# Hybrid decoder layer on Trainium2: laying the queries out through DRAM instead of by many small copies

## What is computed

```python
z = u @ w_in
qa, ka, va, qn, kc, vc, ksl, vsl, kw, vw, g_nsa, g_merge = jnp.split(z, cuts, axis=-1)
qa = rope(heads_q(qa, A_KV_HEADS, A_REP), pos)
ka = rope(heads_kv(ka, A_KV_HEADS), pos)
oa = banded_attention(qa, ka, heads_kv(va, A_KV_HEADS), A_WINDOW, sinks...)
qn_rot = rope(qn, pos)
kcmp = compress(heads_kv(kc, ...), ...)      # gelu(flat @ w1 + b1) @ w2
vcmp = compress(heads_kv(vc, ...), ...)
o_cmp, p_cmp = compressed_attention(qn, kcmp, vcmp)
idx = select_blocks(p_cmp)
o_slc = selected_attention(qn_rot, rope(ksl), vsl, idx)
o_win = banded_attention(qn_rot, rope(kw), vw, B_WINDOW, None)
y = gm[:, :, 0] * (oa @ w_proj_a) + gm[:, :, 1] * (ob @ w_proj_b)
h  = layer_norm(ALPHA * x + y @ w_out)
x' = layer_norm(ALPHA * h + (silu(h @ w_gate) * (h @ w_up)) @ w_down)
```

## Time and profile before

| | |
|---|---|
| runs of the kernel | 4864.35, 4977.32, 5441.69 us (median 4977.32) |
| profiled execution, time | 4870.62 us |
| profiled execution, span of the slowest core (core 6) | 4869.6 us |
| spans of all cores | 4842.0 to 4869.6 us |
| mean granted TensorE clock | 0.972 to 0.975 of full speed |
| busy, share of the span | PE 88%, weight loads 43%, DVE 41%, ACT 36%, POOL 20% |
| DMA | 413 MB, mean 85 GB/s |

### The profile page before, as it was taken

The page is one execution under the profiler, slowest core; times in us unless marked ns, Lnnn a source line. Parts: engine busy times, 40 slices in busy tenths (PEclk is TensorE's granted clock), DMA queues, the critical chain, the costliest instruction groups (busy, mean ns, idle before and its releaser), DMA issues.

```text
span 4869.6 us, 82285 instructions; the slowest of 8 cores (4842.0 to 4869.6 us)
## 1 busy us (share of the span) xinstructions
PE 4304.5 (88%) x27000; PEld 2112.4 (43%) x27000; DVE 2004.3 (41%) x4848; ACT 1746.9 (36%) x2186; POOL 989.3 (20%) x891
## 2 busy tenths in 40 slices
PE   2777899899987889999997789999999688999998
PEld 1344444344444444444443444444444344444444
DVE  0554455232355445523145544542325544453323
ACT  0158723211125862321122685331111388333111
POOL 1431112210243111102034210210114311121101
PEclk6899999999999999999999999999999999999999
DMA  7240133945222011253421101234432110124231
GB/s 126 76 106 14 24 107 94 213 125 156 81 71 74 2 53 53 93 165 89 131 80 54 61 2 53 78 104 139 129 97 86 46 46 2 74 74 156 89 122 45
DMA packets 207375, 412.99 MB, mean 85 GB/s; under 512 B 33008, under 2 KB 80496, under 8 KB 203760
## 3 DMA queue, kind: packets, MB, share of 16 engines
q1 hardware_dynamic: 173952, 356.97, 22.0%
q0 software_dynamic: 33008, 50.77, 6.9%
HBM read 327.79 MB, written 99.14 MB: 88 GB/s over the span
## 4 chain that ended last, share of the span: by engine, by line
PE 71%; ACT 8%; DMA 5%; SPq 5%; DVE 5%; issue 4%; POOL 1%; DVEq 0%; POOLq 0%; ACTq 0%
PE bpair L317 23%; PE bpair L318 12%; PE bpair L315 9%; ACT pt L340 7%; SPq L156 5%; PE bpair L316 5%; PE bpair L302 4%; PE bpair L307 4%; PE bpair L314 4%; PE bpair L309 2%; PE bpair L308 2%; PE bpair L335 1%; DMA ffr<-wu 1%; PE bpair L312 1%; DVE pre L344 1%
## 5 line engine op out<-in xcount | busy, mean ns | idle before, releaser
L317 PE MATMUL bpair<-hT,ffr 128*128 128x512 bf16 x5632 | 1229.9, 380 | 24.5 <-DMA ffr<-wg 17.3
L340 ACT ACTIVATE pt<-bpair 128x1024 bf16<-128x1024 f32 (+1 forms) x1016 | 991.9, 1018 | 230.3 <-PE bpair L313 129.3
L317 PEld LDWEIGHTS bpair<-hT,ffr 128*128 128x128 bf16 x5632 | 549.7, 98 | 691.0 <-issue 38.7
L344 DVE TENSOR_TENSOR actf<-sgt,bpair 128x512 bf16<-128x512 f32 x352 | 240.8, 688 | 914.3 <-PE bpair L317 896.2
L318 PE MATMUL bpair<-Wd,actf 128*128 128x512 bf16 x2816 | 609.1, 379 | 0.0
L340 ACT ACTIVATE sgt<-bpair 128x512 f32<-128x512 f32 x352 | 207.7, 596 | 834.0 <-PE bpair L317 833.5
L315 PE MATMUL bpair<-xT,wgm 128*128 128x512 bf16 x2048 | 488.8, 382 | 0.0
L318 PEld LDWEIGHTS bpair<-Wd,actf 128*128 128x128 bf16 x2816 | 275.5, 98 | 332.2
L302 PE MATMUL bpair<-xT,w 128*128 128x512 bf16 x1664 | 393.9, 393 | 28.5 <-DVE t L344 14.1
L307 PE MATMUL bpair<-Qr,Ksl 128*128 128x512 bf16 x1088 | 344.9, 387 | 75.9 <-ACT pt L340 49.8
L344 POOL TENSOR_TENSOR sb_lnst<-sb_lnst,sb_mhalf 128x1 f32<-128x1 f32 x128 | 70.2, 549 | 1501.3 <-DVE sb_lnst L350 1501.3
(11 more groups left out here) (130 smaller groups left out, 4589.1 us busy)
## 6 DMA issues: line engine op xcount, KB each, us to landing
ffr<-wg_b SPq DMA_DIRECT2D x154, 256.0 KB, 3.0
ffr<-wu_b SPq DMA_DIRECT2D x154, 256.0 KB, 3.2
pre<-x SPq DMA_DIRECT2D x64, 512.0 KB, 3.8
hs<-pre SPq DMA_DIRECT2D x64, 512.0 KB, 2.6
H<-hs SPq DMA_DIRECT2D x64, 512.0 KB, 4.3
out<-H SPq DMA_DIRECT2D x64, 512.0 KB, 2.6
Wd<-wd_b SPq DMA_DIRECT2D x66, 256.0 KB, 4.5
xT<-xt POOLq DMA_DIRECT2D x16, 1024.0 KB, 12.5
```

The source lines that it names most:

```text
L317: "gu": lambda *a, **k: t.matmul(*a, **k),
L340: return self.s.op("act", lambda: nc.scalar.activation(out=out, in_=in_, func=func, **kw), reads, writes, war)
L344: return self.s.op(eng, lambda: e.tensor_tensor(out=out, in0=in0, in1=in1, op=op), reads, writes, war, out.shape[0])
```

## The change

Five edits: the queries of both mixers go, tile by tile of 128x512, into a DRAM tensor `qd` and are read back from it in the wanted layout, one write and one read where there were four copies (`lay_out`); the Bufs of `QaT`, `Qn` and `Qr` are split by half; mixer A's key copies are issued by ACT, with a Buf `b_ka` of their own; `compress1` runs behind each of the first four pairs of query projections instead of behind every second; the sinks have a Buf of their own, and their exponential stands behind the keys of the first sequence.

```diff
-            dsems = {q: [... for i in range(16)] for q in ("sp", "pool")}
+            dsems = {q: [... for i in range(16)] for q in ("sp", "pool", "act")}
...
+        self.qd = self.nc.dram_tensor("qd", [48, 128, 512], BF16, kind="Internal").ap()
+        self.b_qd = [Buf("qd%d" % i) for i in range(48)]
...
-        s.dma("sp", (self.esink[:], dr["sinks"]), writes=[bc])
-        self.act(self.esink[:], self.esink[:], AF.Exp, [bc], [bc])
+        self.b_sink = Buf("sink")
+        s.dma("sp", (self.esink[:], dr["sinks"]), writes=[self.b_sink])
...
+    def lay_out(self, place, src, bs, dst, b_dst):
+
+        self.s.dma("sp", (self.qd[place], src), reads=[bs], writes=[self.b_qd[place]])
+        self.s.dma("sp", (dst, self.qd[place].rearrange("(j p) t -> p j t", j=4)), reads=[self.b_qd[place]],
+                   writes=[b_dst])
...
-            prs = []
-            for h in range(2):
-                for g in range(2):
-                    prs.append((self.KaT[64 * g + 32 * h:64 * g + 32 * h + 32, g, ts_], o[h][32 * g:32 * g + 32, :]))
-                    prs.append((self.Ksl[32 * h:32 * h + 32, g, ts_], o[h][64 + 32 * g:96 + 32 * g, :]))
-            s.dma("sp", prs, reads=bo, writes=[self.b_k1[tc]])
+            hg = [(h, g) for h in range(2) for g in range(2)]
+            s.dma("sp", [(self.Ksl[32 * h:32 * h + 32, g, ts_], o[h][64 + 32 * g:96 + 32 * g, :]) for h, g in hg],
+                  reads=bo, writes=[self.b_k1[tc]])
+            s.dma("act", [(self.KaT[64 * g + 32 * h:64 * g + 32 * h + 32, g, ts_], o[h][32 * g:32 * g + 32, :])
+                          for h, g in hg], reads=bo, writes=[self.b_ka[tc]])
...
         if not self.cbias_done:
             self.cbias_done = True
+            self.act(self.esink[:], self.esink[:], AF.Exp, [self.b_sink], [self.b_sink])
...
-                s.dma("sp", [(self.QaT[64 * g + 32 * h:64 * g + 32 * h + 32, j, ts_], o[h][32 * j:32 * j + 32, :])
-                             for h in range(2) for j in range(4)], reads=bo, writes=[self.b_qa[g][tc]])
-                if g == 1:
-                    compress1(tc // 2, tc % 2)
+                for h in range(2):
+                    self.lay_out(8 * g + 2 * tc + h, o[h][:], bo[h], self.QaT[64 * g + 32 * h:64 * g + 32 * h + 32, :, ts_],
+                                 self.b_qa[g][tc][h])
+                if tc < 2:
+                    compress1(tc, g)
...
-            s.dma("sp", [(self.Qn[64 * g + 32 * h:64 * g + 32 * h + 32, j, ts_], zq[h][32 * j:32 * j + 32, :])
-                         for j in range(4)], reads=[b_zq[h]], writes=[self.b_n[g][tc]])
+            self.lay_out(16 + 8 * g + 2 * tc + h, zq[h][:], b_zq[h], self.Qn[64 * g + 32 * h:64 * g + 32 * h + 32, :, ts_],
+                         self.b_n[g][tc][h])
...
-                s.dma("sp", [(self.Qr[g][32 * e:32 * e + 32, j, ts_], o[e][32 * j:32 * j + 32, :])
-                             for e in range(2) for j in range(4)], reads=bo, writes=[self.b_q[g][tc]])
+                for e in range(2):
+                    self.lay_out(32 + 8 * g + 2 * tc + e, o[e][:], bo[e], self.Qr[g][32 * e:32 * e + 32, :, ts_],
+                                 self.b_q[g][tc][e])
```

More of the change, by code:

```diff
@@ L397, in build @@
             sems = {e: E(nc.semaphore("s_" + e)) for e in Sched.ENG}
-            dsems = {q: [E(nc.semaphore("d_%s%d" % (q, i))) for i in range(16)] for q in ("sp", "pool")}
+            dsems = {q: [E(nc.semaphore("d_%s%d" % (q, i))) for i in range(16)] for q in ("sp", "pool", "act")}
             self.s = Sched(nc, sems, dsems)
@@ L572, in phase_p @@
         self.b_one = Buf("one", spans=span(M_V, 12480))
-        self.b_k1 = [Buf("k1_%d" % i, spans=span(M_KA + 1024 * i, 1024, 0, 64) + span(M_KA + 4096 + 1024 * i, 1024, 64, 128)
-                         + strided(M_KS + 1024 * i, 4096, 2, 1024, 0, 64)) for i in range(4)]
+        self.b_ka = [Buf("ka%d" % i, spans=span(M_KA + 1024 * i, 1024, 0, 64) + span(M_KA + 4096 + 1024 * i, 1024, 64, 128))
+                     for i in range(4)]
+        self.b_k1 = [Buf("k1_%d" % i, spans=strided(M_KS + 1024 * i, 4096, 2, 1024, 0, 64)) for i in range(4)]
         self.b_kw = [Buf("kw_%d" % i, spans=strided(M_KW + 1024 * i, 4096, 2, 1024, 0, 64)) for i in range(4)]
@@ L696, in phase_p @@
         self.QaT = self.at("QaT", M_QA, [128, 4, S], BF16)
-        self.b_qa = [[Buf("qa%d%d" % (g, i), spans=strided(M_QA + 1024 * i, 4096, 4, 1024, 64 * g, 64 * g + 64))
-                      for i in range(4)] for g in range(2)]
+        self.b_qa = [[[Buf("qa%d%d" % (g, i), spans=strided(M_QA + 1024 * i, 4096, 4, 1024, 64 * g + 32 * h, 64 * g + 32 * h + 32))
+                       for h in range(2)] for i in range(4)] for g in range(2)]
         wA = [self.next_w() for _ in range(4)]
@@ L732, in phase_p @@
         self.Qr = [self.at("Qr%d" % g, (M_QR0, M_QR1)[g], [128, 4, S], BF16) for g in range(2)]
-        self.b_n = [[Buf("n%d%d" % (g, i), spans=strided(M_QN + 1024 * i, 4096, 4, 1024, 64 * g, 64 * g + 64))
-                     for i in range(4)] for g in range(2)]
-        self.b_q = [[Buf("q%d%d" % (g, i), spans=strided((M_QR0, M_QR1)[g] + 1024 * i, 4096, 4, 1024, 0, 64))
-                     for i in range(4)] for g in range(2)]
+        self.b_n = [[[Buf("n%d%d" % (g, i), spans=strided(M_QN + 1024 * i, 4096, 4, 1024, 64 * g + 32 * h, 64 * g + 32 * h + 32))
+                      for h in range(2)] for i in range(4)] for g in range(2)]
+        self.b_q = [[[Buf("q%d%d" % (g, i), spans=strided((M_QR0, M_QR1)[g] + 1024 * i, 4096, 4, 1024, 32 * h, 32 * h + 32))
+                      for h in range(2)] for i in range(4)] for g in range(2)]
         self.b_pad = [Buf("pad%d" % g, spans=span((M_QR0, M_QR1)[g], 16384, 64, 128)) for g in range(2)]
@@ L812, in pvf @@
             self.tt(den, pv[:, :, 64], self.esink[:, 4 * g:4 * g + 4], ALU.add,
-                    [self.b_bank[pv_i], self.b_const], [self.b_small])
+                    [self.b_bank[pv_i], self.b_sink], [self.b_small])
             rden = self.small[:, 4:8]
@@ L925, in score_unit @@
                 self.mm("sc", stb[:], kcmp[:, g, :], Qn[:, :, qs], True, False,
-                        [self.b_kcmp, b_n[0][qt // 4], b_n[1][qt // 4]], bb)
+                        [self.b_kcmp] + b_n[0][qt // 4] + b_n[1][qt // 4], bb)
                 self.mm("mask", stb[:], self.ident[:], self.cmpbias[:, qs].unsqueeze(1).to_broadcast([128, 4, 128]),
@@ L938, in score_unit @@
                 self.mm("ss", stb[:], Ksl[:, g, ks], Qr[:, :, qs], True, msk is None,
-                        [self.b_k1[kt // 4], self.b_eblk, self.b_kpad, b_q[g][qt // 4], b_aug[g][qt], self.b_pad[g]], bb)
+                        [self.b_k1[kt // 4], self.b_eblk, self.b_kpad, b_aug[g][qt], self.b_pad[g]] + b_q[g][qt // 4], bb)
             else:
                 self.mm("sw", stb[:], KwT[:, g, ks], Qr[:, :, qs], True, msk is None,
-                        [self.b_kw[kt // 4], self.b_kpad, b_q[g][qt // 4], b_aug[g][qt], self.b_pad[g]], bb)
+                        [self.b_kw[kt // 4], self.b_kpad, b_aug[g][qt], self.b_pad[g]] + b_q[g][qt // 4], bb)
             if msk is not None:
```

2 lines of the change are left out of this document (1 added, 1 removed).

## The result

Timed in turns against the kernel before on one chip, the changed kernel takes 0.9932 of its time, with a 95% interval of 0.9903 to 0.9961. The profiled execution spans 4830.5 us on its slowest core (core 5, all cores 4800.4 to 4830.5), against 4869.6: 39 us less. The forecast was 76 us less, 4795. The direction was right, half the gain is missing (by the ratio the gain is 33 us). The whole is within the 2% that count as no change here. Three timings of the changed kernel came to 4826.9, 4831.5 and 4838.2 us, so two spans that differ by less than some 10 us are told apart only by their stretches.

A forecast was written before the change was run, and what follows sets the result against it. TensorE was busy 88%, but SP's DMA issuing held it up before and in mixer A. Savings of 17 us in each of three sequences (51) plus 25 in the first made 76, from 4870.6 to 4795; range 4760 to 4866.

The forecast's parts named there:

- the mark: Start of mixer B's scores, 3883.5 in the fourth sequence; forecast 17.0 us earlier there, 25 us in the first sequence.
- L = 2.2: Landing time of a 128 KB query-tile write to DRAM: 2.2 us, so a tile costs SP 2.70 us.
- S = 3751: Fourth sequence: SP takes up the queries at about 3751 instead of 3759.8, ACT issuing four of eight key copies; 8.8 us.
- M = S + 5.25 + 10c + L: Start of mixer B's scores, 3866.5 against 3883.5; c, SP's time per `(g, tc)` of queries, is 10.8 us (before 12.05).
- First sequence, S = 173: SP's queries in the first sequence begin at 173 instead of 187.8; the mark comes at 288.5 against 313.7, 25 us.
- After it nothing is touched, so a shift of the mark is a shift of the end.: Stretches behind the mark stay unchanged to 1 us, so its 17 us, 25 in the first sequence, reach the end.
- What is gained in mixer A's stage is the Buf that was split.: Mixer A's stage: the second `Qn` group's 1.8 us wait goes; halving the number of issues buys nothing by itself.
- Compression: Fourth sequence: DVE's 3.4 us products move up, first four pairs cost 5.8 each; first score at 3777.5, not 3790.7.
- A wait of the first query pairs for DVE: Sign in the projection stage that would make the mechanism wrong: the first query pair waiting for DVE; no size given.
- Sinks: First sequence: the wait for the exponential and its load, from 102.2 to 108.3, is saved: 6 us.
- gain given back: Rival, chance 0.10: writes land in 2.6 us; mixer A's gain is lost, 0.6 a sequence, 8.6 in the first; 4860.
- slower: Rival, chance 0.05: the write's round trip on SP becomes the bound; gain gone at 2.66 us landing, 4975 at 3.3.

The follow-up runs named there:

- keys_back: Changed kernel with all eight key copies issued by SP again; span 4858.3 us against 4830.5, ratio to the kernel before 0.9997.
- twice: Changed kernel with every tile of `Qr` written to DRAM twice, the second write waiting for the first; span 4921.1 us against 4830.5.
- late_w: Changed kernel with the loads of the weights behind mixer B begun 14 units later, in the first sequence alone; span 4822.0 us against 4830.5.
- copies_back: Changed kernel with the four 32-row copies per tile again instead of a DRAM write and read; span 4813.2 us against 4830.5.
- pipe: Changed kernel with both writes of a pair issued before both reads; span 4784.8 us against 4830.5.
- split_only: Kernel before with only the queries' Bufs split by halves and the sinks' load on its own Buf; lowest time 4836.1 us against 4862.8.
- comp_back: Changed kernel with the compressions again behind every second pair of query projections; span 4827.3 us against 4830.5.
- gel3: Changed kernel with three DVE steps instead of four in each compression; span 4830.2 us against 4830.5.

## Why the prediction was half right

The forecast of 76 us and the measured 39 differ by 37. By the table these are 14 in mixer B of the first sequence, 2 behind it, 8 at the mark of the first sequence, and 13 in the other three (51 forecast, 38 measured). Two steps failed: what follows the mark was taken as untouched, and S was put too early. A third, that SP's queue sets the mark, was wrong too but cost little.

- *L = 2.2.* Near enough. Writes land in 2.0 us (median over all) and the reads in 2.2; a tile takes 2.73 among the queries of mixer A and 2.59 among mixer B's, up to the mark of the fourth sequence, against 2.70. The estimate of 2.3 for 128 KB that goes by the Trainium skill ("DMA: Bandwidth & Descriptors", section "Anatomy of one DMA — SWDGE (gpsimd) path") is 0.3 above the median; that section is on DMAs issued by GpSimd, and these are SP's. Neither figure holds where other transfers load the DMA engines (8.6 to 10.3 us).
- *S = 3751.* Wrong in its size, and the term that cost most in sequences 2 to 4. The places of the marks, in us (the forecast is one for all three; the first row counts from L302):

| | forecast | 2 | 3 | 4 |
|---|---|---|---|---|
| S | 48.7 | 50.2 | 51.7 | 53.2 |
| S to SP's first `zr` write | 43.2 | 44.1 | 45.2 | 43.7 |
| from there to the mark | 72.3 | 74.8 | 73.4 | 74.2 |

Of the 17.9 us by which the three marks come late S has 9.0. (The balance above has 13: the kernel before was 3 us slower in its second and third sequence together than the forecast took it to be, and 2 us were won behind the marks.) The forecast let the turn of an `o` set, 6.4 us per two key steps, be the bound and left out TensorE's projections, which allow two steps of the first keys in 6.9 at best; with the waits for landings at the window keys two steps take 7.4 in the mean (fourth sequence). The four weight loads take 2.72 and not 1.76. What ACT took over is nevertheless worth 27 to 28 us by `keys_back`. The Trainium skill ("DMA: Bandwidth & Descriptors", section "Issuing engines are not separate DMA queues") calls such a saving "usually small" beside the DMA itself; here an issue is 0.64 us beside a landing of 1.8, and it was not small.
- *M = S + 5.25 + 10c + L, "the queue, not TensorE, sets it".* The mechanism is wrong for the changed kernel, and its number is near by luck. By its rows SP's seventh `(g, tc)` begins at 3832.79, from which the formula has the mark at 3840.2; it stands at 3844.7. SP sets the third cast, and behind it TensorE's own 5.4 us a cast do the rest. Two of these are 10.8, just what the forecast had for c, so the error is only the 1 to 2.5 us in the table's last row. Where SP is slower (`twice`) the formula comes out on the measured mark.
- *First sequence, S = 173.* The first write is issued at 174.8, nearly right, but lands at 183.4, 8.6 us later. Just ahead of it SP issued write-backs of converted weights (`wfm_b<-w`, one of which takes 8.8 to land), and SP's own queue holds the DMA engines 76% of the time there (174.5 to 184); no converting load runs. The forecast counted the landing as L everywhere.
- *"After it nothing is touched, so a shift of the mark is a shift of the end."* Wrong in the first sequence, and the costliest step: 14 us. The layouts end after the mark, when `wgm` is already loading, and the last two writes take 10.3 and 8.7 us to land instead of 2.0. `late_w`, `copies_back` and `pipe` each bring B1 back to 273 or 274.
- *"What is gained in mixer A's stage is the Buf that was split."* Right, and shown alone: 25 us in `split_only`. In the changed kernel it isn't there: A has an earlier start, but SP arrives late (3770.5 where 3752.4 is TensorE's start), so the time gained in front is waited for behind, with a projection at half the clock on top. `comp_back` shows the same exchange from the other side (Q +4.2, A -5.4), `pipe` ends it.
- *Compression.* The chain was put at 3.4 us and is 4.1; its neighbour POOL was left out of the price. A wait of the first query pairs for DVE was named as what would make the mechanism wrong. It is there, but the time doesn't hang on it: `gel3` shortens it from 3.97 to 2.94 us and gains nothing, as SP is next.
- *Sinks.* The start moved by 6.2 us, as forecast (kernels with the edit begin L302 at 113.5 to 119.2, those without at 123.1 and 123.6). How much of it reaches the end is open.

The rival *gain given back* (4860) had the right sense of it, that mixer A gains nothing, but for another reason: not a slower L, but SP's late arrival at mixer B's queries. The *slower* rival's mechanism is real (`twice`); its long landings are met only where other transfers load the DMA engines.

## What to carry to other kernels

If an engine that issues DMAs waits for each landing in turn, issue first everything that doesn't depend on a landing: two writes and then two reads were worth 41 (lowest times) to 46 us (spans) here, where the same layout in the order write, read, write, read was worth nothing. A buffer that is read by a DMA is held for the landing, so before a transfer is counted at its quiet price, look at what else is loading at that very moment, and at who waits behind the one that reuses the buffer. And where removing one bound gains nothing, remove the next with it before calling the first one false.

## What was not expected of the hardware

- Two DVE steps of 128x254 float32 between SBUF tiles took 1.25 and 1.29 us beside POOL's sums, where one took 0.41 just before; products that read PSUM (128x512) stayed at 0.68.
- The issue of a copy of 32x512 between SBUF tiles took 0.59 us, that of a write of 128x512 to DRAM, four times the bytes, 0.33.
- Two writes of 128 KB issued back to back landed in the same 2.0 us as single ones (`pipe`).
- A 128 KB write beside converting loads on POOL's queue landed in 8.7 and 10.3 us.
